# Opening of a hybrid decoder trunk: x through one DMA queue, the first two weight chunks through the other

## The reference

```python
def hybrid_layer(x, g, w_in, ...):
    h = rmsnorm(x, g)
    z = h @ w_in                     # w_in is 1024 x 2840
    u_lru, g_lru, q, g_nsa, kc, vc, ks, vs, kwn, vwn, gate_logits = jnp.split(z, splits, axis=-1)
    ...                              # RG-LRU group and native sparse attention group
    return x + y @ w_out
```

## Time and profile before

| | us |
|---|---|
| median of 3 runs | 555.83 |
| lowest, highest | 555.33, 557.75 |
| profiled execution, its time | 555.62 |
| profiled execution, its span | 553.8 |
| TensorE busy | 539.1 (97% of the span) |
| VectorE busy | 394.7 (71%) |
| ScalarE busy | 294.2 (53%) |
| GpSimd busy | 43.7 (8%) |

### The profile page before, as it was taken

How to read it: one execution, slowest core, us unless ns; L and a number is a source line. 1 busy time by engine, 2 the same in 40 slices (tenths; PEclk the granted TensorE clock), 3 DMA queues, 4 the chain that set the end, 5 groups by cost and what they waited for, 6 DMA issues and landing times.

```text
span 553.8 us, 8602 instructions
## 1 busy us (share of the span) xinstructions
PE 539.1 (97%) x3171; PEld 400.8 (72%) x3171; DVE 394.7 (71%) x651; ACT 294.2 (53%) x592; POOL 43.7 (8%) x86
## 2 busy tenths in 40 slices
PE   6999999999999999999999999999999999999995
PEld 5777868778767766668887787777877776776674
DVE  4686996689976778656737499668977687587542
ACT  4847735625755465543634773572475454455532
POOL 3001100130000000000520110013000000000000
PEclk9999999999999999999999999999999999999999
DMA  9858465365111111012333856627422112000013
GB/s 265 222 150 212 97 167 109 79 146 137 51 48 30 38 39 40 5 35 76 79 96 95 212 127 152 125 58 151 98 74 78 39 39 49 28 2 1 1 38 113
DMA packets 92040, 49.91 MB, mean 90 GB/s; under 512 B 40912, under 2 KB 90208, under 8 KB 92000
## 3 DMA queue, kind: packets, MB, share of 16 engines
q1 hardware_dynamic: 89376, 45.17, 32.2%
q0 software_dynamic: 1536, 3.15, 2.3%
q10 hardware_dynamic: 1088, 1.06, 0.6%
HBM read 44.12 MB, written 2.10 MB: 83 GB/s over the span
## 4 chain that ended last, share of the span: by engine, by line
PE 77%; DVE 13%; issue 4%; ACT 3%; DMA 1%; POOL 1%; POOLq 0%; DVEq 0%; ACTq 0%
PE z_ps L1491 12%; PE z_ps L1493 11%; PE z_ps L1492 11%; PE t_ps L1591 7%; PE s_ps L1567 6%; PE o_ps L1627 5%; PE a_ps L1627 4%; PE o_ps L1491 3%; PE o_ps L1493 3%; PE o_ps L1492 3%; DVE w_lo L1119 2%; DVE probs L1273 2%; PE t_ps L1601 1%; PE t_ps L1596 1%; DMA swp<-E 1%
## 5 line engine op out<-in xcount | busy, mean ns | idle before, releaser
L1055 ACT ACTIVATE probs<-s_ps,mn 128x128 f32<-128x128 f32 (+3 forms) x128 | 66.6, 526 | 72.1 <-DVE mn L1389 70.7
L1491 PE MATMUL z_ps<-h_hi,w_hi 128*128 128x512 f32 x248 | 101.5, 409 | 1.3 <-issue 0.9
L1493 PE MATMUL z_ps<-h_hi,w_lo 128*128 128x512 f32 x248 | 97.0, 391 | 0.0
L1492 PE MATMUL z_ps<-h_lo,w_hi 128*128 128x512 f32 x248 | 96.8, 390 | 0.0
L900 ACT ACTIVATE w_hi<-stage 128x1024 fp32r<-128x1024 f32 x56 | 59.2, 1058 | 58.7 <-PE z_ps L1493 36.2
L1119 DVE TENSOR_TENSOR w_lo<-stage,w_hi 128x1024 fp32r<-128x1024 f32 x56 | 68.3, 1220 | 7.8 <-ACT w_hi L900 7.0
L1389 DVE TENSOR_REDUCE mn<-s_ps 128x1 f32<-128x384 f32 (+3 forms) x88 | 52.3, 635 | 28.1 <-PE s_ps L1575 27.9
L1491 PEld LDWEIGHTS z_ps<-h_hi,w_hi 128*128 128x128 f32 x248 | 46.6, 188 | 15.5 <-issue 5.5
L1493 PEld LDWEIGHTS z_ps<-h_hi,w_lo 128*128 128x128 f32 x248 | 46.6, 188 | 10.2
L1492 PEld LDWEIGHTS z_ps<-h_lo,w_hi 128*128 128x128 f32 x248 | 46.7, 188 | 8.5 <-issue 0.2
L1398 DVE COPY probsT<-t_ps 128x512 f32<-128x512 f32 (+1 forms) x48 | 32.8, 684 | 22.1 <-PE t_ps L1591 21.8
(11 more groups left out here) (235 smaller groups left out, 915.2 us busy)
## 6 DMA issues: line engine op xcount, KB each, us to landing
stage<-in_w_in SPq DMA_DIRECT2D x28, 512.0 KB, 4.5
stage<-in_w_in SPq DMA_DIRECT2D x32, 256.0 KB, 3.8
stage<-in_cmp_k_w SPq DMA_DIRECT2D x8, 512.0 KB, 3.8
stage<-in_cmp_v_w SPq DMA_DIRECT2D x8, 512.0 KB, 4.2
stage<-in_w_out SPq DMA_DIRECT2D x8, 512.0 KB, 3.5
stage<-in_w_out SPq DMA_DIRECT2D x16, 256.0 KB, 3.8
swp<-E POOLq DMA_DIRECT2D x48, 64.0 KB, 2.3
out<-xT SPq DMA_DIRECT2D x8, 256.0 KB, 2.4
```

What stands on the lines that cost most here:

```text
L1055: act.activation(probs[:, 4 * pair + 2 * g + r, c0:c0 + W], s_ps[g][:, at * W:(at + 1) * W], ACT.Exp, scale=-1.0, bias=mn[:, m % 2, g, at: ...
L1491: pe.matmul(bank, w_hi[:, slot, at:at + P], x_hi, start=first, stop=False)
L1492: pe.matmul(bank, w_hi[:, slot, at:at + P], x_lo, start=False, stop=False)
L1493: ins = pe.matmul(bank, w_lo[:, slot, at:at + P], x_hi, start=False, stop=last)
```

## The change

x parts 1 and 3 are issued by SyncE, which issues all four parts in order and then chunk 2. Chunks 0 and 1 are issued by ScalarE, with a new helper that does for these two what `load` does: chunk 0 behind `norm_g`, chunk 1 behind the small activation. The semaphores and destinations stay the same.

```diff
+        def first_load(eng, n):
+            key = plan.loads[n]
+            at = {"kc": COL_KC, "vc": COL_VC}[key[2]]
+            eng.dma_start(stage_of(key).rearrange("p (k n) -> p k n", k=KT),
+                          w_in[key[1]].rearrange("(k p) n -> p k n", p=P)[:, :, at:at + P]).then_inc(staged[n % N_STAGE], 16)
...
-            x_part(sync, 0)
-            load(0)
-            x_part(sync, 2)
-            load(1)
+            for c in range(TT):
+                x_part(sync, c)
             load(2)
...
             act.dma_start(par_row[PG:PG + DEPTH * KT, :], norm_g.rearrange("l (m p) -> (l m) p", p=P)).then_inc(norm_in, 16)
-            x_part(act, 1)
-            x_part(act, 3)
+            first_load(act, 0)
             act.wait_ge(first_consts, 1)
             act.activation(table[:, :], ones[:, 0:1], ACT.Copy)
+            first_load(act, 1)
             act.wait_ge(a_dve, 1)
```

## The result

The change makes the kernel slower by 0.31%: 557.98 us (median of 14 runs, 557.35 to 559.85) against 556.38 us for the kernel before in the same measurement (14 runs), a ratio of 1.0031 with a 95% interval of 1.0021 to 1.0042, which is 1.2 to 2.3 us. That is within the 0.5% that were named as no change. But it is a loss clear of noise, and its median lies above the forecast range of 554.8 to 557.8 us.

What follows compares the result with a forecast made beforehand. TensorE, busy 97% of 553.8 us, bounds the kernel, so opening delays pass one to one. Chunk 0 +0.2 us, the rest 0: span 554.0 us, execution 555.8 us, median 556.0 us; range 554.8 to 557.8 us.

Steps and rivals of the forecast that it cites:

- The chain: Waits through the opening, from warm-up transposes to VectorE's copies and splits until 18.01 us, said to hold no transfer.
- the covers: Time to spare between a transfer's landing and its need in the opening, 0.7 to 1.3 us in the kernel before.
- rival 3: Opening: the wait for x part 1 was on the path; 1.0 us earlier gives 1.0 us, 554.8 us; chance 0.05.
- Rival 2: ScalarE held in issuing chunk 1, so late at h_hi of tile 0; costs 1.6 or 3.6 us; chance 0.10.
- The start of that chunk isn't in the trace: Chunk 0 on ScalarE's queue: start taken as 3.5 us, landing 9.0 us, a cost of 0.2 us.
- x part 1's descriptors at a rate: Making x part 1's 512 descriptors ahead of chunk 0 takes 0.9 us, so chunk 0 starts at 2.6 + 0.9 = 3.5 us.
- The upper bound, 9.95 us: Latest landing forecast for chunk 0, from a start at 4.45 us, at a cost of 1.2 us.
- a need at 8.78 us: When ScalarE, done with the two h_hi, takes up chunk 0; 0.7 us to spare in the kernel before.
- turn x part 1 earlier: TensorE's transposes in the opening: x part 1 lands at 8.1 us, 1.0 us earlier, worth 0.

Runs made afterwards that it cites:

- the filled wait: The changed kernel with 22 and then 8 more identity transposes on TensorE in its wait for chunk 0: 557.70 us, 1.0021 times the kernel before.
- second profile of the kernel before: The kernel before, run again with nothing changed, for another profile: 0.9999 times the kernel before.
- norm_g on SyncE: The changed kernel with norm_g issued by SyncE ahead of x part 0, so chunk 0 is first on ScalarE's queue: 1.0010 times the kernel before.

## Why the prediction was wrong, point by point

The chain and the covers were read rightly. Chunk 0 was the one transfer that counted; split_hi(0) and split_lo(0) held up all behind them; x part 1's wait was worth nothing (rival 3 is out); a delay at w_lo went through one to one along VectorE's list. Chunk 1 landed at 1.90 + 12.5 = 14.4 us and was in time. Rival 2 is out: ScalarE's second issue was over at 2.52 us.

The step that failed is the landing of chunk 0 in the part "The start of that chunk isn't in the trace": 3.5 + 4.4 + 1.1 = 9.0 us. Measured is 10.4 us. The start was after 4.4 us and not at 3.5 us, 1.0 us of the miss: I charged it with x part 1's descriptors at a rate, as 0.9 us, where the runs show that any further part on SyncE's queue holds it to 4.4 us. The transfer went at 220 packets per us and not 233, which makes 1024/220 = 4.65 us, 0.25 us more. The rest, some 0.1 us, is the tail to the landing. The upper bound, 9.95 us, used the right start with the two other terms too small, and counted from a need at 8.78 us where the timeline has 8.68 us: a cost of 1.2 us, where w_lo came 1.7 us later. The median of the kernel before is also 0.55 us higher over 14 runs than over the first three, and the two together put the result 0.2 us above the range.

A second term was priced at nothing because it wasn't thought of: TensorE's clock. I noted that TensorE would turn x part 1 earlier and called that worth 0. With the chunk late as well, it left TensorE idle for 3.7 us in one piece, where before there were 2.1 and 0.9 us with transposes between, and the clock was lowered after it. That cost 0.63 us in one profile of the changed kernel and 0.57 us in the other, and 0.6 us between the medians with and without the filled wait.

## What to carry to other kernels

Order the transfers of an opening by when they are needed, over both queues together: a transfer at the head of a second queue isn't ahead of the first queue's backlog, it starts late and then shares every second packet with it. Here it was enough to put the needed chunk behind x part 0 on the same queue, or to issue x parts 2 and 3 some us later. TensorE's idle time in an opening can cost clock, and with it time that no wait shows; in two cases transposes of no use in that wait were worth 0.6 and 0.8 us between medians. What makes the clock fall these runs don't settle: it isn't only idle time in one piece, for it stayed up behind idle stretches of 1.30 and 1.72 us (second profile of the kernel before) and fell behind stretches of 1.21 and 1.80 us (norm_g on SyncE).

## What the runs showed of the hardware that was not expected

- The hold between the two queues works both ways. With x part 0 first, chunk 0's first packets came after 4.4 us (issued at 1.28 us); with chunk 0 first, x part 0's came after 3.6 us (issued at 1.25 us).
- ScalarE's queue issued chunk 1 at 1.90 us, while its table load ran from 1.83 to 3.11 us: an issue behind an activation in the program didn't wait for it.
- The end of the same 20 warm-up transposes came at 5.8 and 5.9 us in the profiles of the kernel before and at 6.4 us in one of the changed kernel (1.84 + 4.53), with nothing changed ahead of them on TensorE. So single profiles of an opening differ by 0.6 us at its first step, and landings compare better than starts.
- A lower clock in the opening needn't show where one looks first: in one profile VectorE's list took 9.56 us all the same, and the 0.63 us came out 7 us further on, at an instruction of ScalarE that waits for TensorE.
